# Inverses of an RWKV scan kept as packed 32-wide blocks, with the last level joining them to 64

## Chip, cores and metric

One NeuronCore of a Trainium2 chip runs the whole kernel as one launch. The metric is device time in microseconds.

## What is computed

The kernel runs a network of three blocks on 256 tokens of width 1024, in float32. The change lies in the second block's RWKV-7 mixer, with 16 heads of 64 features. What its scan must compute, cut to the core:

```python
def rwkv7_scan(r, decay, k, v, a, b):
    """State S[v_i, k_j]: S <- S diag(w) + (S a) b^T + v k^T ; y = S r."""
    def step(state, inp):
        r_t, w_t, k_t, v_t, a_t, b_t = inp
        sa = jnp.einsum('bhij,bhj->bhi', state, a_t)
        state = (state * w_t[:, :, None, :] + sa[..., None] * b_t[:, :, None, :]
                 + v_t[..., None] * k_t[:, :, None, :])
        y = jnp.einsum('bhij,bhj->bhi', state, r_t)
        return state, y
    _, y = lax.scan(step, s0, (r, decay, k, v, a, b))
```

The mixer calls it with `a = -kk` and `b = kk * a_rate`.

## The kernel before

The scan isn't stepped token by token. The 256 tokens are cut into four spans of 64. Within a span the rows `sa` depend on each other through a strictly triangular 64x64 matrix per head, and the kernel multiplies by the inverse of identity minus that matrix. There are 16 heads times 4 spans, so 64 such inverses. Two of them (two spans of one half of the tokens) lie above each other on the 128 partitions.

Inverses are made by doubling (`pe_double_a`, `pe_double_b`, L2254 to L2266; `dve_double_a`, `dve_double_b`, L2269 to L2280). The start is the inverse of the 2x2 blocks on the diagonal, `X`, and its transpose, `Y`. Level n joins blocks of size 2, 4, 8, 16 and 32 (`BLOCKS_64`) in three products: `between` is Lb by X, VectorE masks it into `T`; then `wider` is Y by T and is added to X, and `wider_turned` is T by Y and is added to Y. The last level makes only `wider_turned`, because the scan reads only `Y`. All products are 64x64 by 64x64, on full matrices that are zero outside their blocks.

The heads go in four groups of four, `pp` = 0 to 3. One call of `pe_blocks` (L2240) makes one product for one group: 16 calls of `mm`, over pair of heads q, token half b, head hd and span H, where H gives both the rows read and the partitions written. A float32 `mm` is two weight loads and two matmuls in the trace, so a call is 32 MATMUL and 32 LDWEIGHTS. The order is written by hand in `DOUBLING` (L2284): first product of group pp, then second and third of group pp-1, and so on, with four `bonus` products of another sum (L2295) put in between. All engines follow the same list, or their own share of it, in program order.

Ahead of it stand the pair products: `dve_front` (L2139) scales the operands, `pe_pairs` (L2159) makes Lb and Lk (64x128 each) and the 64x64 product for X, `dve_pairs` (L2198) masks them, GpSimd adds the unit diagonals (`pool_scan`, L2462), `pe_by_token` (L2224) transposes. Behind it `pe_span` (L2361) goes through the four spans one after the other and reads Y. TensorE, ScalarE and VectorE meet at the end of the scan (`all_drained`).

The trace names tiles by buffer: `rwkv_e_cum` holds X, `rwkv_e_neg_cum` holds Y, `rwkv_log_decay` holds T, `rwkv_pairs_b` is Lb. `L105` is the helper of all matmuls.

In block 3 another mixer has products of narrow tiles, that read 64 partitions, write 32 and have 32 columns (`pe_level`): 32 calls of `mm` for one level, so 64 MATMUL, with a wait only ahead of a level. `pe_mixers` has four such levels in a row (`LOW[0:4]`), and later two more.

## Time and profile before

| what | value |
|---|---|
| median of 3 runs | 3142.64 us (3137.49 to 3145.12) |
| the profiled execution | 3145.6 us, span 3143.8 us |
| TensorE | 2974.6 us busy (95%), 23720 MATMUL |
| weight loads | 2762.0 us busy, 23720 LDWEIGHTS |
| VectorE | 1718.4 us busy (55%) |
| ScalarE | 1435.3 us busy (46%) |
| GpSimd | 160.9 us busy (5%) |
| mean granted TensorE clock | 0.968 of full |

The RWKV scan takes the time from about 2338 us to 2464 us of the span: the pair products to 2369.9 us, the doubling to 2426.2 us, the spans to 2464.4 us. The rest of the kernel is large matrix products, which aren't touched.
### The profile page before, as it was taken

How to read it: one execution, taken by the hardware profiler on the slowest of the kernel's cores; microseconds unless marked ns; L12 is line 12 of the kernel's file. 1: busy time of each engine (PE TensorE's matmuls, PEld its weight loads, DVE VectorE, ACT ScalarE, POOL GpSimd, SP SyncE). 2: the span in 40 equal slices, each digit the busy share in tenths (PEclk: the TensorE clock that was granted, in tenths of full speed). 3: DMA queues.
4: the chain of work that ended last, by engine and by line, in shares of the span. 5: the costliest groups of instructions: out<-in, count | busy, mean ns of one | idle time of the engine just before them, and what ended most of it. 6: DMA issues, size and time to landing. Idle time of an engine off the chain costs nothing.

```text
span 3143.8 us, 53947 instructions
## 1 busy us (share of the span) xinstructions
PE 2974.6 (95%) x23720; PEld 2762.0 (88%) x23720; DVE 1718.4 (55%) x2029; ACT 1435.3 (46%) x1831; POOL 160.9 (5%) x197
## 2 busy tenths in 40 slices
PE   8998898999998898999999999999889999999998
PEld 8988898999988898998989899898879899886887
DVE  5464555545554555545555645545676454464555
ACT  4455655445455655444445444444451344344444
POOL 1000100000000100001000000000011000044000
PEclk9999999999999999999999999999889999898999
DMA  6553334554553334555554445454320155440453
GB/s 244 188 181 120 122 137 159 188 188 174 188 185 123 122 136 154 187 188 210 186 201 163 157 179 188 177 186 172 134 81 4 70 187 186 145 162 22 158 183 134
DMA packets 69395, 492.89 MB, mean 157 GB/s; under 512 B 7854, under 2 KB 9422, under 8 KB 10535
## 3 DMA queue, kind: packets, MB, share of 16 engines
q1 hardware_dynamic: 64224, 465.53, 41.2%
q10 hardware_dynamic: 4938, 23.92, 2.0%
q8 instruction: 188, 3.08, 0.4%
q14 instruction: 45, 0.36, 0.0%
HBM read 488.32 MB, written 1.06 MB: 156 GB/s over the span
## 4 chain that ended last, share of the span: by engine, by line
PE 80%; DVE 8%; ACT 6%; POOL 2%; issue 2%; PEld 1%; DMA 0%; PEldq 0%; ACTq 0%; DVEq 0%; POOLq 0%; SPq 0%
PE bank L105 52%; PE acc L105 28%; DVE weights_lo L313 2%; ACT weights_hi L118 2%; POOL conv_gate L3073 1%; POOL conv_out L3076 1%; DVE tmp L671 1%; DVE h L664 1%; DVE h L679 1%; PEld acc L105 0%; DVE b_x_lo L503 0%; PE acc L999 0%; DVE b_x_lo L731 0%; ACT L1067 0%; ACT L1133 0%
## 5 line engine op out<-in xcount | busy, mean ns | idle before, releaser
L313 DVE TENSOR_TENSOR weights_lo<-weight_ring,weights_hi 128x2048 fp32r<-128x2048 f32 x440 | 1009.6, 2295 | 944.8 <-ACT weights_hi L118 944.4
L105 PE MATMUL bank<-b_x_hi,weights_hi 128*128 128x256 f32 x3576 | 1015.8, 284 | 21.7 <-DVE b_x_lo L731 16.9
L105 PE MATMUL bank<-b_x_hi,weights_lo 128*128 128x256 f32 x3576 | 1011.1, 283 | 0.0
L118 ACT ACTIVATE weights_hi<-weight_ring 128x2048 fp32r<-128x2048 f32 x440 | 839.5, 1908 | 375.6 <-PE acc L105 364.7
L105 PE MATMUL bank<-b_x_lo,weights_hi 128*128 128x256 f32 x3576 | 1010.6, 283 | 0.0
L105 PEld LDWEIGHTS bank<-b_x_hi,weights_hi 128*128 128x128 f32 x3576 | 679.7, 190 | 34.3 <-issue 18.9
L105 PEld LDWEIGHTS bank<-b_x_lo,weights_hi 128*128 128x128 f32 x3576 | 680.0, 190 | 3.3
L105 PEld LDWEIGHTS bank<-b_x_hi,weights_lo 128*128 128x128 f32 x3576 | 679.1, 190 | 0.0
L105 PE MATMUL acc<-weights_hi,b_hidden_hi 128*128 128x512 f32 x832 | 329.5, 396 | 0.0
L105 PE MATMUL acc<-weights_hi,b_hidden_lo 128*128 128x512 f32 x832 | 328.2, 394 | 0.0
L105 PE MATMUL acc<-weights_lo,b_hidden_hi 128*128 128x512 f32 x832 | 327.5, 394 | 0.0
L118 ACT ACTIVATE b_hidden_hi<-act_gate 128x256 fp32r<-128x256 f32 x208 | 86.9, 418 | 340.0 <-DVE act_gate L888 312.4
L864 ACT ACTIVATE act_gate<-bank 128x256 f32<-128x256 f32 x176 | 67.6, 386 | 281.1 <-PE bank L105 280.9
L105 PEld LDWEIGHTS acc<-weights_hi,b_hidden_lo 128*128 128x128 f32 x832 | 156.5, 188 | 37.7
L105 PEld LDWEIGHTS acc<-weights_lo,b_hidden_hi 128*128 128x128 f32 x832 | 156.7, 188 | 32.8
L105 PEld LDWEIGHTS acc<-weights_hi,b_hidden_hi 128*128 128x128 f32 x832 | 156.5, 188 | 32.7 <-DVE weights_lo L313 0.4
L105 PE MATMUL bank<-weights_hi,b_x_hi 128*128 128x256 f32 (+2 forms) x528 | 152.8, 289 | 9.2 <-DVE weights_lo L313 7.6
L105 PE MATMUL bank<-weights_lo,b_x_hi 128*128 128x256 f32 (+2 forms) x528 | 152.4, 289 | 0.0
L105 PE MATMUL bank<-weights_hi,b_x_lo 128*128 128x256 f32 (+2 forms) x528 | 152.2, 288 | 0.0
L105 PE MATMUL acc<-b_x_hi,weights_hi 128*128 128x256 f32 x416 | 123.8, 298 | 16.5 <-ACT tmp L1067 11.3
L891 DVE TENSOR_TENSOR b_hidden_lo<-act_gate,b_hidden_hi 128x256 fp32r<-128x256 f32 x176 | 75.3, 428 | 85.2 <-ACT b_hidden_hi L118 85.2
L105 PE MATMUL acc<-b_x_lo,weights_hi 128*128 128x256 f32 x416 | 120.0, 289 | 0.0
(487 smaller groups left out, 4029.7 us busy)
## 6 DMA issues: line engine op xcount, KB each, us to landing
weight_ring<-in_weights SPq DMA_DIRECT2D x440, 1024.0 KB, 4.8
xn<-in_norm_rows ACTq DMA_DIRECT2D x14, 1024.0 KB, 4.8
sgu_bias_row<-in_sgu_rows ACTq DMA_DIRECT2D x1, 2048.0 KB, 10.8
sgu_norm_rows<-in_sgu_rows ACTq DMA_DIRECT2D x1, 2048.0 KB, 9.7
bias_hankel<-bias_scratch ACTq DMA_DIRECT2D x1, 1536.0 KB, 7.0
h<-in_x SPq DMA_DIRECT2D x2, 512.0 KB, 6.6
mem_norm<-in_memory SPq DMA_DIRECT2D x1, 1024.0 KB, 13.8
sgu_w_spatial<-in_sgu_w_spatial ACTq DMA_DIRECT2D x1, 1024.0 KB, 4.8
```

Source lines behind the costliest of these rows:

```text
L105: return pe.matmul(out, a, b, start=start, stop=stop, skip_group_check=True)
L118: return act.activation(out, in_, ACT.Copy, scale=scale)
L313: dve.tensor_tensor(k.w.lo[:, n % 2, :], k.ring[:, n % RING, :], k.w.hi[:, n % 2, :], ALU.subtract) \
L664: dve.scalar_tensor_tensor(out=h, in0=h, scalar=alpha / scale, in1=acc_of(k, b), op0=ALU.mult, op1=ALU.add, accum_out=stat(k, 0, b)).then_ ...
L671: dve.scalar_tensor_tensor(out=k.t[:, b], in0=k.h[:, b, :], scalar=stat(k, 1, b), in1=k.rows[:, 0], op0=ALU.add, op1=ALU.mult).then_inc(*k ...
L679: dve.scalar_tensor_tensor(out=half(k.h[:, b], i), in0=half(k.t[:, b], i), scalar=stat(k, 6, b), in1=half(k.rows[:, 1], i), op0=ALU.mult, ...
L864: act.activation(k.act_gate[:, c, :], k.bank[c][:, 0:S], ACT.Silu).then_inc(*k.s.up("silu", f, j, c))
L891: dve.tensor_tensor(k.hid.lo[:, j % 2, c, :], k.act_gate[:, c, :], k.hid.hi[:, j % 2, c, :], ALU.subtract) \
L3073: pool.tensor_scalar(k.conv_sg[:, 1, :], k.conv_in[:, 1, j:j + S], k.col(("conv_dw_w_3", (0, j)), 1), None, ALU.mult).then_inc(*k.s.up("po ...
L3076: pool.tensor_tensor(k.conv[:, 1, :], k.conv[:, 1, :], k.conv_sg[:, 1, :], ALU.add) \
```

## The change

`X`, `Y` and `T` are kept as packed 32x32 blocks: four blocks above each other on the partitions (`R4`), so X and Y together fill one buffer (`XY`, where X alone was), and T half of its old one. `pe_pairs` makes both start products as 32x32 tiles over 64 features (`pairs_32`, 64 calls of `mm` per group where `pairs_turned` had 16), VectorE masks them in one operation per head, and Y no longer comes from Lb. Levels n = 0 to 3 run all three products on 32x32 blocks, four `mm` per (q, b, hd) where there were two; VectorE's operations have 256 columns instead of 512. A last level (`last_a`, `last_b`) takes the quarter of Lb below the diagonal, multiplies it on both sides (two `mm` per (q, b, hd)), and the result is copied with the diagonal blocks into a full 64x64 transposed inverse `Y_64`, which lies in Y's old buffer and is zeroed by GpSimd before. ScalarE, VectorE and GpSimd share these copies. `pe_span` reads `Y_64`, and waits for the last of the copies just before the first use.

The diff, with unchanged lines left out:

```diff
+    "scalar_last": ("diagonal_act", "below_act", "right_act"),
+    "vector_last": ("below_dve", "right_dve", "mask_pairs"),
+    "gpsimd_last": ("unit_diagonal", "no_left", "diagonal_pool"),
...
-    mats["identity_64"] = i == j
...
-    mats["pairs_down"] = (i // 2 == j // 2) & (i > j)
-    mats["pairs_up"] = (i // 2 == j // 2) & (i < j)
-    for n in BLOCKS_64:
+    i, j = row % 32, np.arange(32)[None, :]
+    mats["identities_32"] = np.concatenate([i == j, i == j], axis=1)
+    mats["pairs_32"] = np.concatenate([(i // 2 == j // 2) & (i > j), (i // 2 == j // 2) & (i < j)], axis=1)
+    for n in BLOCKS_32:
...
-BLOCKS_64 = (2, 4, 8, 16, 32)
+BLOCKS_32 = (2, 4, 8, 16)
...
-    k.X, k.Y = by_head(k.eL[:, :, :]), by_head(k.emL[:, :, :])
+    k.XY = by_head(k.eL[:, :, :])
+    k.X, k.Y = k.XY[:, :, :, :, 0:32], k.XY[:, :, :, :, 32:64]
+    k.Y_64 = by_head(k.emL[:, :, :])
...
-    k.T = by_head(ld.rearrange("p (q t) -> p q t", q=KT))
+    k.T = ld[:, 1024:].rearrange("p (q b h t) -> p q b h t", q=KT, b=NB, h=2)
...
-        outs = [empty(k, pe, bank + hd, ("mask_up" if of == "b" else "mask_k", pp, hd))
+        outs = [empty(k, pe, bank + hd, ("mask_" + of, pp, hd))
...
-    outs = [empty(k, pe, hd, ("mask_down", pp, hd))[:, 0:S].rearrange("p (q b t) -> p q b t", q=2, b=NB)
+    outs = [empty(k, pe, hd, ("mask_pairs", pp, hd))[:, 0:S].rearrange("p (q b i t) -> p q b i t", q=2, b=NB, i=2)
...
-    for q in range(2):
-        for c in range(4):
-            b, H, T = span(c)
-            for hd in range(2):
-                a = mm(pe, outs[hd][H, q, b, :], k.rw["kk"][F2[hd], 2 * pp + q, T], k.rw["b"][F2[hd], 2 * pp + q, T],
-                       q + b == 0, True)
-    a.then_inc(*k.s.up("pairs_turned", pp))
-def identities(k, n):
-    return k.con("identity_64").unsqueeze(1).to_broadcast([P, n, 64])
+    kk, bb = k.rw["kk"], k.rw["b"]
+    for i, (x, y) in enumerate(((kk, bb), (bb, kk))):
+        for q in range(2):
+            for b in range(NB):
+                for R, T in tiles_32(b):
+                    for hd in range(2):
+                        a = mm(pe, outs[hd][R, q, b, i, :], x[F2[hd], 2 * pp + q, T], y[F2[hd], 2 * pp + q, T],
+                               i + q + b == 0, True)
+    a.then_inc(*k.s.up("pairs_32", pp))
+R4 = [slice(32 * r, 32 * r + 32) for r in range(4)]
+def tiles_32(b):
+    return [(R4[r], slice(b * P + 32 * r, b * P + 32 * r + 32)) for r in range(4)]
...
 def mask_64(k, name, n):
...
-        dve.tensor_tensor(one_half(k.Y, pp, hd), lb[:, :, 0:64], mask_64(k, "pairs_up", 4), ALU.mult) \
-            .then_inc(*k.s.up("mask_up", pp, hd))
...
-    dve.wait_ge(*k.s.at("pairs_turned", pp))
+    dve.wait_ge(*k.s.at("pairs_32", pp))
...
-        dve.tensor_tensor(one_half(k.X, pp, hd), k.bank[hd][:, 0:S].rearrange("p (n t) -> p n t", n=4),
-                          mask_64(k, "pairs_down", 4), ALU.mult).then_inc(*k.s.up("mask_down", pp, hd))
+        dve.tensor_tensor(one_half(k.XY, pp, hd), k.bank[hd][:, 0:S].rearrange("p (n i) -> p n i", n=4),
+                          mask_64(k, "pairs_32", 4), ALU.mult).then_inc(*k.s.up("mask_pairs", pp, hd))
...
 def of_two(x, pp):
...
-def pe_blocks(k, pe, bank, pp, mark, taken, lhs, rhs, *ready):
-    out = empty(k, pe, bank, taken).rearrange("p (q b h t) -> p q b h t", q=2, b=NB, h=2)
+def pe_blocks(k, pe, bank, pp, mark, taken, lhs, rhs, *ready, rows=R4, to=R4):
+    out = empty(k, pe, bank, *taken)[:, 0:S].rearrange("p (q b h t) -> p q b h t", q=2, b=NB, h=2)
...
-                for H in F2:
-                    a = mm(pe, out[H, q, b, hd, :], lhs(2 * pp + q)[H, b, hd, :], rhs(2 * pp + q)[H, b, hd, :],
+                for n, (R, O) in enumerate(zip(rows, to)):
+                    a = mm(pe, out[O, q, b, hd, :], lhs(2 * pp + q, n)[R, b, hd, :], rhs[R, 2 * pp + q, b, hd, :],
...
 def pe_double_a(k, pe, n, pp):
...
-    pe_blocks(k, pe, pp % 2, pp, ("between", n, pp), ("between_masked", n, pp), lambda px: k.Lb[:, px, :, :, 0:64],
-              lambda px: k.X[:, px], inverse(n, pp))
+    pe_blocks(k, pe, pp % 2, pp, ("between", n, pp), (("between_masked", n, pp),),
+              lambda px, r: k.Lb[:, px, :, :, 32 * (r % 2):32 * (r % 2) + 32], k.X, inverse(n, pp))
...
 def pe_double_b(k, pe, n, pp):
...
-    if n < len(BLOCKS_64) - 1:
-        pe_blocks(k, pe, 2 + pp % 2, pp, ("wider", n, pp), ("inverse", n + 1, pp), lambda px: k.Y[:, px],
-                  lambda px: k.T[:, px], ("between_masked", n, pp))
-    pe_blocks(k, pe, 4 + pp % 2, pp, ("wider_turned", n, pp), ("inverse_turned", n + 1, pp), lambda px: k.T[:, px],
-              lambda px: k.Y[:, px], ("between_masked", n, pp), *((("inverse_turned", n, pp),) if n else ()))
+    pe_blocks(k, pe, 2 + pp % 2, pp, ("wider", n, pp), (("inverse", n + 1, pp),), lambda px, r: k.Y[:, px], k.T,
+              ("between_masked", n, pp))
+    pe_blocks(k, pe, 4 + pp % 2, pp, ("wider_turned", n, pp), (("inverse_turned", n + 1, pp),),
+              lambda px, r: k.T[:, px], k.Y, ("between_masked", n, pp), *((("inverse_turned", n, pp),) if n else ()))
+def pe_last_a(k, pe, n, pp):
+    pe_blocks(k, pe, pp % 2, pp, ("below", pp), (("below_act", pp), ("below_dve", pp)),
+              lambda px, r: k.Lb[:, px, :, :, 32:64], k.X, inverse(N_DOUBLE, pp), rows=R4[0::2], to=R4[1::2])
+def pe_last_b(k, pe, n, pp):
+    pe_blocks(k, pe, 4 + pp % 2, pp, ("right", pp), (("right_act", pp), ("right_dve", pp)), lambda px, r: k.T[:, px],
+              k.Y, ("below_act", pp), ("below_dve", pp), ("inverse_turned", N_DOUBLE, pp), rows=R4[1::2], to=R4[0::2])
+def in_half_bank(bank):
+    return bank[:, 0:S].rearrange("p (n t) -> p n t", n=8)
...
 def dve_double_a(k, dve, n, pp):
...
-    dve.tensor_tensor(of_two(k.T, pp), k.bank[pp % 2].rearrange("p (n t) -> p n t", n=8),
-                      mask_64(k, f"down_{BLOCKS_64[n]}", 8), ALU.mult).then_inc(*k.s.up("between_masked", n, pp))
+    dve.tensor_tensor(of_two(k.T, pp), in_half_bank(k.bank[pp % 2]), mask_64(k, f"down_{BLOCKS_32[n]}", 8), ALU.mult) \
+        .then_inc(*k.s.up("between_masked", n, pp))
...
 def dve_double_b(k, dve, n, pp):
...
-        if come == "wider_turned" or n < len(BLOCKS_64) - 1:
-            dve.wait_ge(*k.s.at(come, n, pp))
-            dve.tensor_tensor(of_two(x, pp), of_two(x, pp), k.bank[bank + pp % 2].rearrange("p (n t) -> p n t", n=8),
-                              ALU.add).then_inc(*k.s.up(mark, n + 1, pp))
+        dve.wait_ge(*k.s.at(come, n, pp))
+        dve.tensor_tensor(of_two(x, pp), of_two(x, pp), in_half_bank(k.bank[bank + pp % 2]), ALU.add) \
+            .then_inc(*k.s.up(mark, n + 1, pp))
+def act_last_a(k, act, pp):
+    act.wait_ge(*k.s.at("inverse_turned", N_DOUBLE, pp))
+    for r in range(2):
+        copy_act(act, of_two(k.Y_64[:, :, :, :, 32 * r:32 * r + 32], pp)[R4[r]], of_two(k.Y, pp)[R4[r]]) \
+            .then_inc(*k.s.up("diagonal_act", pp, r))
+    act.wait_ge(*k.s.at("below", pp))
+    copy_act(act, of_two(k.T, pp)[R4[1]], in_half_bank(k.bank[pp % 2])[R4[1]]).then_inc(*k.s.up("below_act", pp))
+def act_last_b(k, act, pp):
+    act.wait_ge(*k.s.at("right", pp))
+    copy_act(act, of_two(k.Y_64[:, :, :, :, 32:64], pp)[R4[0]], in_half_bank(k.bank[4 + pp % 2])[R4[0]]) \
+        .then_inc(*k.s.up("right_act", pp))
+def act_last(k, act):
+    act.wait_ge(*k.s.at("no_left"))
+    for pp in range(4):
+        act_last_a(k, act, pp)
+        if pp:
+            act_last_b(k, act, pp - 1)
+    act_last_b(k, act, 3)
+def dve_last_a(k, dve, n, pp):
+    dve.wait_ge(*k.s.at("below", pp))
+    dve.tensor_copy(of_two(k.T, pp)[R4[3]], in_half_bank(k.bank[pp % 2])[R4[3]]).then_inc(*k.s.up("below_dve", pp))
+def dve_last_b(k, dve, n, pp):
+    if not pp:
+        dve.wait_ge(*k.s.at("no_left"))
+    dve.wait_ge(*k.s.at("right", pp))
+    dve.tensor_copy(of_two(k.Y_64[:, :, :, :, 32:64], pp)[R4[2]], in_half_bank(k.bank[4 + pp % 2])[R4[2]]) \
+        .then_inc(*k.s.up("right_dve", pp))
+def pool_diagonals(k, pool):
+    pool.wait_ge(*k.s.at("bonus_gated", 3))
+    for pp in range(4):
+        pool.wait_ge(*k.s.at("inverse_turned", N_DOUBLE, pp))
+        for r in range(2):
+            pool.tensor_copy(of_two(k.Y_64[:, :, :, :, 32 * r:32 * r + 32], pp)[R4[2 + r]],
+                             of_two(k.Y, pp)[R4[2 + r]]).then_inc(*k.s.up("diagonal_pool", pp, r))
+            pool.wait_ge(*k.s.at("diagonal_pool", pp, r))
+N_DOUBLE = len(BLOCKS_32)
...
-for _n in range(len(BLOCKS_64)):
+for _n in range(N_DOUBLE + 1):
...
-        DOUBLING.append(("a", _n, _pp))
+        DOUBLING.append(("a" if _n < N_DOUBLE else "last_a", _n, _pp))
...
-            DOUBLING.append(("b", _n - (_pp == 0), (_pp - 1) % 4))
-DOUBLING.append(("b", len(BLOCKS_64) - 1, 3))
+            _m = _n - (_pp == 0)
+            DOUBLING.append(("b" if _m < N_DOUBLE else "last_b", _m, (_pp - 1) % 4))
+DOUBLING.append(("last_b", N_DOUBLE, 3))
...
 def pe_span(k, pe, c):
...
+    if not c:
+        for m in (("right_act", 3), ("right_dve", 3), ("diagonal_pool", 3, 1)):
+            pe.wait_ge(*k.s.at(*m))
...
-            a = mm(pe, cols64(out, px)[H], k.Y[H, px, b, i, :], cols64(k.R[i], px)[H], px == 0, True)
+            a = mm(pe, cols64(out, px)[H], k.Y_64[H, px, b, i, :], cols64(k.R[i], px)[H], px == 0, True)
...
-        {"a": pe_double_a, "b": pe_double_b, "bonus": pe_bonus}[half](k, pe, n, pp)
+        {"a": pe_double_a, "b": pe_double_b, "last_a": pe_last_a, "last_b": pe_last_b, "bonus": pe_bonus}[half](k, pe, n, pp)
...
-    pe.wait_ge(*k.s.at("inverse_turned", len(BLOCKS_64), 3))
...
+    act_last(k, act)
...
-        {"a": dve_double_a, "b": dve_double_b, "bonus": dve_bonus}[half](k, dve, n, pp)
+        {"a": dve_double_a, "b": dve_double_b, "last_a": dve_last_a, "last_b": dve_last_b, "bonus": dve_bonus}[half](k, dve, n, pp)
...
 def inverse(n, pp):
-    return ("inverse", n, pp) if n else ("unit_diagonal", pp, "X")
+    return ("inverse", n, pp) if n else ("unit_diagonal", pp)
...
 def pool_scan(k, pool):
...
-        for x, name, come in ((k.Y, "Y", "mask_up"), (k.X, "X", "mask_down")):
-            pool.wait_ge(*k.s.at(come, pp, 1))
-            pool.tensor_tensor(of_two(x, pp), of_two(x, pp), identities(k, 8), ALU.add) \
-                .then_inc(*k.s.up("unit_diagonal", pp, name))
+        pool.wait_ge(*k.s.at("mask_pairs", pp, 1))
+        pool.tensor_tensor(of_two(k.XY, pp), of_two(k.XY, pp), mask_64(k, "identities_32", 8), ALU.add) \
+            .then_inc(*k.s.up("unit_diagonal", pp))
+    pool.memset(k.emL[:, :, :], 0.0).then_inc(*k.s.up("no_left"))
...
+    pool_diagonals(k, pool)
...
```

## Rows read from the trace of the kernel before

**Rows 1.** Busy time, granted clock and DMA by stage.

```profile
core 0: us, PE busy (x) PEld busy (x) DVE busy (x) ACT busy (x) POOL busy (x), PEclk, DMA share, GB/s
...
2340.00:2369.80 29.80, 21.66 (x432) 19.33 (x432) 25.55 (x54) 6.16 (x12) 11.23 (x8) 0.79 0.07 28
2369.80:2426.20 56.40, 56.40 (x1777) 54.45 (x1776) 39.98 (x58) 4.72 (x10) 5.10 (x4) 1.00 0.02 4
2426.20:2464.40 38.20, 36.45 (x937) 35.78 (x933) 10.36 (x16) 7.13 (x12) 0.00 (x0) 1.00 0.01 3
```

**Rows 2.** The chain that ended last: start us, us, what.

```profile
2358.02 0.60 DVE rwkv_pairs_b L2202
2358.62 0.33 DVE rwkv_e_neg_cum L2204
2358.95 0.60 DVE rwkv_pairs_b L2202
2359.55 0.34 DVE rwkv_e_neg_cum L2204
2359.89 0.14 issue
2360.03 3.69 PE acc L105 x64
2363.72 0.85 PE bank L105 x32
...
2369.95 3.11 PE bank L105 x96
2373.07 0.93 PE acc L105 x32
2374.00 1.87 PE bank L105 x64
...
2379.60 0.93 PE bank L105 x32
2380.53 1.06 PE acc L105 x4
...
2459.82 1.87 PE bank L105 x32
```

**Rows 3.** Groups by form in the doubling: busy us, mean ns, idle before.

```profile
L105 PE MATMUL bank<-rwkv_e_cum,rwkv_pairs_b 64*64 64x64 f32 x640 | 22.0, 218 | 0.0
...
L2271 DVE TENSOR_TENSOR rwkv_log_decay<-bank,cons 128x512 f32<-128x512 f32 x20 | 13.8, 692 | 9.8 <-PE bank L105 9.8
L2279 DVE TENSOR_TENSOR rwkv_e_neg_cum<-rwkv_e_neg_cum,acc 128x512 f32<-128x512 f32 x20 | 13.8, 689 | 5.0 <-PE acc L105 5.0
...
L2321 POOL TENSOR_TENSOR tmp<-tmp,rwkv_gate 128x512 f32<-128x512 f32 x4 | 5.1, 1274 | 32.7 <-ACT tmp L2313 32.7
```

**Rows 4.** Groups of VectorE by form in the pair products.

```profile
L2202 DVE TENSOR_TENSOR rwkv_pairs_b<-acc,cons 128x512 f32<-128x512 f32 x8 | 5.4, 679 | 0.3 <-PE acc L105 0.3
...
L2204 DVE TENSOR_TENSOR rwkv_e_neg_cum<-acc,cons 128x256 f32<-128x256 f32 x8 | 3.3, 410 | 0.0
L2212 DVE TENSOR_TENSOR rwkv_e_cum<-bank,cons 128x256 f32<-128x256 f32 x8 | 3.0, 409 | 0.0
```

**Rows 5.** Timeline of TensorE in block 3: start us, us, what.

```profile
2889.65 0.76 PE L105 MATMUL bank<-hgrn_q,hgrn_k 64*32 64x32 f32 x64
2890.26 1.69 PE L105 MATMUL bank<-xn 64*32 64x32 f32 x164
2893.96 0.34 PE L105 MATMUL bank<-xn 64*32 64x32 f32 x28 [2.01 <-issue]
2894.30 0.61 PE L105 MATMUL acc<-cmp_w_by_key,cmp_v 15*64 15x256 f32 x2
...
2901.65 0.81 PE L105 MATMUL bank<-xn 64*32 64x32 f32 x64 [0.36 <-issue]
2902.32 0.75 PE L105 MATMUL bank<-tmp 64*32 64x32 f32 x64
2903.03 0.39 PE L105 MATMUL acc<-tmp 64*64 64x64 f32 x6
```

**Rows 6.** What TensorE waited for there.

```profile
PE bank L105 <- issue: 2.0, 1, 2.0
```

**Rows 7.** DMA of that stretch in 40 slices of 0.2 us.

```profile
GB/s 0 0 0 0 0 0 0 0 0 0 82 0 0 0 0 0 0 0 0 0 0 0 0 0 0 0 0 0 0 0 82 0 0 0 0 0 0 0 0 0
DMA packets 2, 0.03 MB, mean 4 GB/s; under 512 B 0, under 2 KB 0, under 8 KB 0
...
q8 instruction: 2, 0.03, 1.9%
```

**Rows 8.** Busy time and granted clock around it.

```profile
2889.60:2892.00 2.40, 2.35 (x230) 2.19 (x229) 2.07 (x6) 2.22 (x3) 0.17 (x1) 1.00 0.03 7
2892.00:2893.96 1.96, 0.00 (x0) 0.00 (x0) 0.88 (x3) 1.93 (x3) 0.00 (x0) 1.00 0.00 0
2893.96:2896.00 2.04, 2.04 (x34) 1.06 (x33) 0.00 (x0) 2.02 (x3) 0.00 (x0) 0.77 0.04 8
2896.00:2900.00 4.00, 4.00 (x13) 2.31 (x12) 0.00 (x0) 0.00 (x1) 0.00 (x0) 0.50 0.00 0
```

**Rows 9.** The two packets of it, in windows of 0.2 us.

```profile
2891.20:2891.40 0.20, 0.20 (x39) 0.20 (x30) 0.20 (x2) 0.20 (x1) 0.00 (x0) 1.00 0.35 82
...
2895.20:2895.40 0.20, 0.20 (x2) 0.19 (x1) 0.00 (x0) 0.20 (x1) 0.00 (x0) 0.50 0.43 82
```

**Rows 10.** DMA queues in the doubling.

```profile
q8 instruction: 14, 0.23, 1.6%
```

**Rows 11.** DMA in 40 slices of 0.25 us, 2371 to 2381.

```profile
GB/s 0 0 0 0 0 0 0 66 0 0 0 0 0 0 0 0 0 0 0 0 0 66 0 33 0 0 0 0 0 0 0 0 0 0 0 0 66 0 0 0
...
q8 instruction: 3, 0.05, 1.9%
```

**Rows 12.** DMA in 40 slices of 0.5 us, 2404 to 2424.

```profile
GB/s 0 0 0 33 0 0 0 0 0 0 33 0 0 0 0 0 0 0 33 0 0 0 0 0 0 33 0 0 0 0 0 0 0 33 0 0 0 0 0 0
DMA packets 5, 0.08 MB, mean 4 GB/s; under 512 B 0, under 2 KB 0, under 8 KB 0
```

**Rows 13.** The page, its queue of instructions.

```profile
q8 instruction: 188, 3.08, 0.4%
```

## The prediction

> **What bounds the kernel now.** I read the page first: TensorE is busy for 95% of the span, so a change in the scan is worth what it does to TensorE's path. Then the busy time by stage: in the doubling (2369.8 to 2426.2 us) TensorE is busy for all 56.40 us at the full clock, VectorE for 39.98 us; in the pair products ahead of it TensorE for 21.66 of 29.80 us and VectorE for 25.55 us [rows 1]. The chain of waits agrees: in the doubling it lies on TensorE alone, 32 matmuls every 0.93 us, and at the end of the pair products on VectorE up to 2359.89 us [rows 2]. VectorE's operations of 692 and 689 ns wait for TensorE each time (9.8 and 5.0 us of idle time in groups of 20) [rows 3]. So the doubling is TensorE's, and its unit is the call: 32 MATMUL in 0.93 us, or 29.2 ns for one. That is the array's pace: a row of 32 matmuls of the same form on one tile (H fixed, both operands there) took 1.87 us, 58.4 ns for one [rows 2], and in the doubling two tiles run side by side.
>
> **What the change asks of TensorE.** Counts, from the code. Before, 56 calls (20 + 16 + 20) of 64 instructions (32 MATMUL and as many weight loads) are 3584, and the four bonus products add 32, so 3616. After: levels 0 to 3 are 4 x 4 x 3 = 48 calls of 32 `mm`, each four instructions: 6144. The last level is 8 calls of 16 `mm`: 512. With the bonus 6688. So the arithmetic falls and the instructions grow by 85%. The start products grow by 48 `mm` in each group, 192 instructions.
>
> *Array time.* The trace has no 32x32 tile. The nearest rows are the narrow products of block 3, with tiles of 64x32 and 32 columns: 64 of them start in 0.61 us (2889.65 to 2890.26), and 164 take 1.69 us less the tail of the last one, about 1.5 us [rows 5]. That is 9.2 to 9.5 ns for one, so a call of 64 would take about 0.60 us instead of 0.93. Four tiles of 32x32 instead of eight of 64x32 might be slower; if only two ran side by side, 14.6 ns for one (half of 29.2) would give 0.93 us again.
>
> *Instruction supply.* The same burst shows what I take for the real bound. Four levels of 64 matmuls stand in a row there, with a semaphore only ahead of each. The timeline has 64 + 164 = 228 of them, then 2.01 us with nothing, then the other 28 [rows 5]. The gap lies 36 matmuls into the fourth level, where the code waits for nothing, and the waits view puts it down to issue [rows 6]; the clock was at full speed when it began [rows 8]. 228 matmuls with their weight loads are 456 instructions. The page has 188 packets of the instruction queue q8 with 3.08 MB, so 16 KB for one [rows 13], and 47,440 matmuls and weight loads on TensorE are 252 for one packet; in the doubling it is (1777 + 1776) / 14 = 254 [rows 1, 10]. So a packet is a block of about 256 instructions of TensorE. In the stretch with the burst there are two packets, at 2891.2 and 2895.2 us [rows 7], each of which took 1.1 to 1.4 us (0.35 and 0.43 of 16 queues for 0.2 us) [rows 9]. My reading: TensorE holds the rest of one block and the next one, a further block is asked for when a block is entered, and it can be used one turnaround later. 456 is the rest of a block, 200, and a whole one. The second block was entered at about 2890.3 us (200 instructions into the burst at 4.7 ns, less what the queue runs ahead), and work went on at 2893.96 us: 3.7 us. In bounds: the two packets of the starved stretch are 4.0 us apart (3.8 to 4.2, slices of 0.2) [rows 7], and in today's doubling, which has no gap, they come 3.5 and 3.75 us apart (slices of 0.25) [rows 11] and on average 3.75 us (30 slices of 0.5 us for four steps) [rows 12]. So the turnaround is between 3.6 and 3.9 us; I take 3.75, near the gapless ones, as 3.7 comes out of the burst too. Today a block of 256 takes the array 128 x 29.2 ns = 3.74 us, just what the supply gives. After the change the array wants it in 128 x 9.4 ns = 1.2 us, and the supply decides.
>
> The Trainium skill ("Runtime: NRT & Kernel Launch", "Instruction fetch mechanics") says that instructions come in 16 KiB blocks of 256, fetched while the current block runs, with only two lines held, and that the fetch is therefore hidden. The block size agrees with the 16 KB of the rows; "hidden" does not agree with the 2.01 us gap. By that sentence the change would be the gain of the first rival.
>
> **The sum**, against the profiled execution of 3145.6 us (span 3143.8), which lies 3 us above the median of 3142.64:
> 1. Doubling. 6688 / 254 = 26.3 blocks. Up to the first boundary about 0.5 us, then 25 turnarounds of 3.75 = 93.75 us, then the rest of the last block at the array's pace, 1.0 us: 95.2 us, for 56.4 now: +38.8. With 3.6 it is 91.5 (+35.1), with 3.9 it is 99.0 (+42.6). The bonus products, 1.06 us each today [rows 2], disappear under it.
> 2. Pair products. VectorE loses the two masks of Y from Lb, 0.33 us each on the chain [rows 2], in each group; the mask of X and Y together has the same 128x256 as that of X alone (409 ns) [rows 4]. TensorE starts the last group when VectorE's masks of the third are done (2359.89): six masks less ahead of it, -2.0. Its start products are 128 narrow matmuls for 32 wide ones of 0.85 us [rows 2]: at 9.4 ns 1.2 us, at twice that, since the clock there is low, 2.4 us; I take +0.5 in all. The 256 instructions more than fit into the time of those groups. Together -1.5, between -2.0 and 0.
> 3. The clock. TensorE would work some 1.2 of each 3.75 us. After the 2 us gap of block 3 the granted clock was 0.77 and then 0.50, the lower level [rows 8]. Inside the doubling that costs nothing (even at 19 ns a block takes 2.4 us). But the spans would begin at the lower level: the first product of 1.87 us [rows 2] and what follows would take twice as long for a few us. +2, between 0 and +3.
> 4. VectorE's operations halve to some 410 ns [rows 4], hidden already. The last level's copies: ScalarE four and VectorE two small ones a group, at most 0.69 us each by the wider rows [rows 3]; a group of the last level has 128 instructions, 1.9 us of supply. GpSimd's eight copies: a 128x512 operation takes it 1.27 us [rows 3], so two copies are 2.6 us at most, and behind the last inverse six calls of 64 instructions (5.6 us) still come before the scan's first product, 1.87 us, and its outputs. Nil; if that cover were gone, up to +2. GpSimd's zeroing of `Y_64` comes before the bonus sums, 50 us early. Nil.
>
> +38.8 - 1.5 + 2 = **+39.3**: 3184.9 us for such an execution, 3182 us against the median.
>
> **Rivals.**
> - *Faster: the supply is no bound* (the gap had another reason, or more blocks are held when the stream is even). Then levels 0 to 3 take 48 x 0.60 = 28.8 us, the last level 8 x 0.47 = 3.7 (32 matmuls at 14.6 ns), the bonus 4.8: 37.3 for 56.4, -19.1, and -1.5: 3142.6 - 20.6 = 3122 us. It decides from a turnaround under 1.2 us. For it: today's doubling shows no gap at all. Against: the gap within a level, and a packet itself takes 1.1 us. Chance 0.13.
> - *A floor for each matmul*, whatever its width. At today's 29.2 ns a call of 64 takes 1.87 us: 48 x 1.87 + 8 x 0.93 + 4.8 = 102 us, +45.6, with -1.5 3187 us. Against it the 9.4 ns of block 3 [rows 5]. Chance 0.06. The Trainium skill ("TensorE: Matmul & The Clock Gate", "Back-to-back issue gap") states a floor of about 25 ns from start to start up to 64 columns; the 9.4 ns don't agree with it, and by it the time of a block would be 3.2 us and still be hidden under the supply.
> - *A deeper store or quicker supply*: four more blocks held at the start, or 2.5 to 3 us for a block when nothing else moves. That takes 10 to 25 us off: 3157 to 3172 us. Chance 0.08.
> - *The change doesn't do what it says*: the 32x32 tiles can't run side by side, or the copies of three engines stall the last level. One tile at a time would be 29.2 ns again, so the time of the second rival or some us more. Chance 0.03.
> - The forecast: 0.70.
>
> **How the numbers follow.** Forecast 3182, its own range 3175 to 3190 from the turnarounds of 3.6 and 3.9 us and the clock. To hold 8 in 10 the range takes in the deeper store and the floor: 3158 to 3196. A measurement of this kernel tells 0.3% (9.4 us) from no change. Faster: the first rival, 0.13. Within 0.3%: 0.03 (a supply so much quicker that it just balances). Slower: 0.84.
>
> **What would show it.** In the doubling: q8 packets 3.6 to 3.9 us apart with some 26 of them; TensorE in bursts of about 128 matmuls in 1.2 us with gaps of about 2.5 us put down to issue, inside calls as well as between them; busy share near a third, a clock that falls to 0.50; VectorE idle for most of it. The whole stage would be 91 to 99 us long. In the pair products the third group's masks should end 2 us sooner. Wrong, if calls of 64 matmuls follow each other every 0.6 us without gaps; then the supply isn't what stopped block 3. Wrong in another way, if the matmuls stand evenly 29 ns apart.

## The result and the profile after

| | before | after |
|---|---|---|
| median | 3141.93 us (3133.12 to 3145.12, 6 runs) | 3209.03 us (3188.01 to 3214.17, 6 runs) |
| the profiled execution, its span | 3145.6 us, 3143.8 us | 3188.01 us, 3186.2 us |
| mean granted clock | 0.968 | 0.957 |

After by before is 1.021 [1.0191, 1.023]: slower by 67 us, above the upper end of the predicted range. On another chip the same pair gave 1.0193 [1.0159, 1.0227] (first experiment below). The page of after, its engines and its queue of instructions (15 packets more than in [rows 13]):

```profile
PE 2978.8 (93%) x25640; PEld 2765.7 (87%) x25640; DVE 1703.8 (53%) x2021; ACT 1439.8 (45%) x1847; POOL 159.6 (5%) x202
...
q8 instruction: 203, 3.33, 0.4%
```

1920 MATMUL more, and TensorE is busy for 4.2 us more only, so the lost time is idle time. The windows of after by stage, with the columns of [rows 1] (pair products, doubling, spans; then the stretch at the lower clock, and what follows it):

```profile
2332.20:2369.80 37.60, 26.09 (x816) 22.58 (x816) 25.54 (x53) 8.29 (x18) 7.16 (x5) 0.76 0.08 31
2369.80:2469.40 99.60, 58.37 (x3345) 51.76 (x3344) 26.01 (x59) 10.65 (x25) 8.24 (x12) 0.59 0.02 4
2469.40:2515.00 45.60, 44.58 (x900) 44.04 (x896) 9.38 (x14) 6.89 (x12) 0.00 (x0) 0.77 0.01 3
2432.00:2490.00 58.00, 40.83 (x1469) 39.53 (x1459) 12.67 (x28) 8.68 (x20) 3.16 (x8) 0.50 0.02 4
2490.00:2515.00 25.00, 23.98 (x618) 23.46 (x616) 6.20 (x9) 4.15 (x7) 0.00 (x0) 0.99 0.01 3
```

The doubling is busy for 58 of 99.6 us where it was busy for 56.40 of 56.40 [rows 1]. With the same boundaries in every trace (from the first scaled copy of VectorE; from the last transpose, the first doubling product; from the first span product; to the last), in us:

| stage | before | after | difference |
|---|---|---|---|
| ahead of the scan | 2337.9 | 2332.2 | -5.7 |
| pair products | 32.0 | 37.6 | +5.6 |
| doubling | 57.4 | 99.6 | +42.2 |
| spans | 36.2 | 45.5 | +9.3 |
| behind the scan | 680.3 | 671.2 | -9.1 |

The scan costs 57 us. The profiled execution was 42.4 us slower because the untouched parts were 14.8 us shorter in it. TensorE's timeline at the start of the doubling and, after the "...", one call further on at the full clock:

```profile
2369.83 1.35 PE L108 MATMUL bank<-rwkv_e_cum,rwkv_pairs_b 32*32 32x32 f32 x128
2371.20 0.71 PE L108 MATMUL bank<-rwkv_log_decay,rwkv_e_cum 32*32 32x32 f32 x60
2374.09 0.26 PE L108 MATMUL bank<-rwkv_log_decay,rwkv_e_cum 32*32 32x32 f32 x4 [2.17 <-issue]
2374.21 1.08 PE L108 MATMUL acc<-rwkv_e_cum,rwkv_log_decay 32*32 32x32 f32 x64
2375.05 1.04 PE L108 MATMUL bank<-rwkv_e_cum,rwkv_pairs_b 32*32 32x32 f32 x59
2377.51 0.32 PE L108 MATMUL bank<-rwkv_e_cum,rwkv_pairs_b 32*32 32x32 f32 x5 [1.42 <-issue]
...
2397.14 0.74 PE L108 MATMUL acc<-rwkv_e_cum,rwkv_log_decay 32*32 32x32 f32 x64
2397.73 0.70 PE L108 MATMUL bank<-rwkv_e_cum,rwkv_pairs_b 32*32 32x32 f32 x49
```

This is the gap of [rows 5], again and again and in the middle of calls. From 2374.09 to the gap there are 4 + 64 + 59 = 127 matmuls, so 254 instructions: one block. A call of 64 starts 0.60 us behind the one before at the full clock (9.3 ns for a matmul) and 0.84 us behind it at the lower one (13.1 ns). A block of 127 matmuls takes the array 1.2 us at the full clock and 1.7 us at the lower one, and the next block comes 3.83 us after the last (below): the array is two to three times as quick as its supply. What TensorE waited for in the doubling, with total, times and longest in us:

```profile
PE bank L108 <- issue: 31.8, 16, 2.6
PE acc L108 <- issue: 8.8, 5, 2.2
PE acc L108 <- DVE rwkv_e_neg_cum L2339: 0.5, 1, 0.5
```

40.6 us of gaps at issue, about all of the stage's idle time. The DMA of 2400 to 2420 us in slices of 0.5 us shows packets 4.0, 4.0, 4.5 and 3.0 us apart; all 26 of the stage come 3.83 us apart on average:

```profile
GB/s 0 0 0 33 0 0 0 0 0 0 0 33 0 0 0 0 0 0 0 33 0 0 0 0 0 0 0 0 33 0 0 0 0 0 33 0 0 0 0 0
DMA packets 5, 0.08 MB, mean 4 GB/s; under 512 B 0, under 2 KB 0, under 8 KB 0
```

### The profile page after: what moved, and what is told of

Same layout as the page of the kernel before. It is cut to its first block, busy times and chain, and to the rows that moved or that the text cites. A ratio compares the mean times of both kernels' runs of the same rounds, so it can differ in the third digit from the quotient of the medians.

```text
span 3186.2 us, 57813 instructions
## 1 busy us (share of the span) xinstructions
PE 2978.8 (93%) x25640; PEld 2765.7 (87%) x25640; DVE 1703.8 (53%) x2021; ACT 1439.8 (45%) x1847; POOL 159.6 (5%) x202
## 3 DMA queue, kind: packets, MB, share of 16 engines
HBM read 488.19 MB, written 1.06 MB: 154 GB/s over the span
## 4 chain that ended last, share of the span: by engine, by line
PE 81%; DVE 8%; ACT 6%; issue 3%; PEld 1%; DMA 0%; POOL 0%; PEldq 0%; ACTq 0%; DVEq 0%; SPq 0%; POOLq 0%
PE bank L108 52%; PE acc L108 28%; DVE weights_lo L316 3%; ACT weights_hi L121 2%; DVE tmp L674 1%; DVE h L667 1%; DVE h L682 1%; PEld acc L108 0%; DVE b_x_lo L734 0%; DVE b_x_lo L506 0%; ACT L1070 0%; PE acc L1002 0%; ACT L1136 0%; DMA weight_ring<-in_weights 0%; ACT tmp L1070 0%
```

## The experiments

**The change again.** After, unchanged, on another chip.

> The changed kernel once more, for a second trace. Stage lengths in the first trace of it: pair products 37.6 us (31.9 before), doubling to the first product of the spans 99.6 us (57.4 before), spans 45.8 us (36.4 before). Supply theory (a block of 256 instructions of TensorE every 3.8 us bounds the doubling): the doubling is 97 to 102 us again, with q8 packets 3.8 us apart on average, and the spans 8 to 11 us longer than before. What the total differs from 3188 us comes from outside the scan, mainly from how long the granted clock is low in block 3. Rival (the supply's turnaround itself varies from run to run): the doubling differs by over 5 us from 99.6 in the direction of the total.

Measured: 3197.02 us (3193.72 to 3214.09, 4 runs) beside 3140.11 (13 runs), 1.0193 [1.0159, 1.0227]. Its trace has 39.1 / 100.3 / 45.3 us for pair products, doubling and spans, and 26 packets 3.83 us apart. The medians differ by 56.9 us and the scans of the traces by 59.1: on this chip the scan is the whole slowdown. The 10 us more of the first chip come up again below.

**Each doubling product in two halves of 32 columns**, in the kernel before: as many instructions as after, the old tiles.

```diff
-                for H in F2:
-                    a = mm(pe, out[H, q, b, hd, :], lhs(2 * pp + q)[H, b, hd, :], rhs(2 * pp + q)[H, b, hd, :],
+                for C in (slice(0, 32), slice(32, 64)):
+                    for H in F2:
+                        a = mm(pe, out[H, q, b, hd, C], lhs(2 * pp + q)[H, b, hd, :], rhs(2 * pp + q)[H, b, hd, C],
```

> The kernel before, with each product of the doubling made as two of 32 columns each: same tiles (64x64), same columns in all, twice the instructions (7168 and 32 of the bonus for 3584 and 32). Result the same. Supply theory: 7200 / 254 = 28.3 blocks at 3.83 us = 107 us for the doubling instead of 57.4, +50 us, and the spans begin at the low clock, +9: +59 us in all. Array theory (only tiles and columns count): +0 to +2 us. A floor of 25 ns for each matmul: 128 x 25... a call of 64 matmuls takes 1.6 us, +37 us, without gaps.

Measured: 3193.03 us (3191.07 to 3196.8), 1.0164 [1.0146, 1.0181]. The doubling took 110.3 us, near what the supply would give, but the timeline says otherwise:

```profile
2371.28 2.03 PE L105 MATMUL bank<-rwkv_log_decay,rwkv_e_neg_cum 64*64 64x32 f32 x64
2373.14 2.03 PE L105 MATMUL acc<-rwkv_e_neg_cum,rwkv_log_decay 64*64 64x32 f32 x64
```

No gap, 64 matmuls every 1.86 us, 29.1 ns for one, as with 64 columns. The clock was full throughout, and the spans kept their 36.2 us. So half the columns save nothing here. What stayed is the weight load of 64 columns, and I take that for the pace; no run shows it by itself. Since 29.2 ns for a matmul is also the pace of the supply, this run does not separate the two. It was a badly chosen one.

**Only the first head of each pair**, in after: half of the doubling's products are left out, so half of the inverses are not made.

```diff
-            for hd in range(2):
+            for hd in range(1):
```

> The changed kernel, with the products of the doubling and of the last level made for one of two heads only (hd 0), so half of the inverses are not made; VectorE's, ScalarE's and GpSimd's work is unchanged. 3360 instructions of TensorE in the doubling for 6688. Supply theory: 13.2 blocks, 12 turnarounds of 3.83 us and 2 to 4 us more: 48 to 51 us for 99.6, so 48 to 52 us off the changed kernel, with gaps put down to issue still in it. Rival (the chain from TensorE to VectorE and back, or the copies of the last level, bound the stage): the chain has as many steps as before, so under 15 us off.

Measured: median 3156.87 us (10 runs: 3140.29 to 3164.47, and one of 3446.37 that the ratio leaves out), 1.0041 [1.0023, 1.0059]; doubling 52.4 us for the 48 to 51 expected. What TensorE waited for in it:

```profile
PE bank L108 <- issue: 11.2, 6, 2.3
PE acc L108 <- issue: 8.8, 4, 2.5
PE acc L108 <- ACT rwkv_log_decay L121: 1.0, 1, 1.0
PE acc L108 <- DVE rwkv_log_decay L2332: 0.7, 1, 0.7
```

The chain of dependent products is as long as in after and the stage is half as long, with 13 packets 3.88 us apart; 1.7 us of waits for the last level's copies now show. A chain through VectorE is out. The kernel as a whole is only some 40 us under the 3197 of after beside it, and the profiled executions differ by 29 us, though the doubling lost 48. The trace shows where a part of that went: the spans took 53.3 us for 45.3. The clock stayed at 0.50 for 38 us of gapless products:

```profile
2429.40:2468.00 38.60, 38.47 (x550) 38.04 (x546) 5.93 (x9) 4.53 (x8) 0.00 (x0) 0.50 0.01 2
```

**Warm products ahead of the spans**, in after: 32 MATMUL of 128x128, which add nothing to the result.

```diff
+    pe_warm(k, pe, 16, 3)
     pe_values_64(k, pe, 0)
```

> The changed kernel with 16 dense products of 128x128 by the identity (results unused) between the last level and the spans, to raise the clock. Theory: the spans were 9.4 us longer only because the granted clock was 0.50 up to 2490 us. The 16 products (64 instructions, 32 matmuls) cost 3.5 to 4 us at the low clock, the clock rises soon after, and the spans take 36.4 to 39 us instead of 45.8: 3 to 6 us off in all, the doubling unchanged. Rival (the low clock stays as long whatever stands there): 4 us more.

Measured: 3195.45 us (3194.52 to 3197.05), 1.017 [1.0154, 1.0187], 1.6 us under after beside it (3193.72 to 3214.09), which is within the spread of the runs, where 3 to 6 us were expected. The timeline, and two windows behind it:

```profile
2473.81 5.57 PE L108 MATMUL bank<-cons 128*128 128x128 f32 x32
2479.30 2.02 PE L108 MATMUL bank<-rwkv_v_by_token,rwkv_pairs_k 64*64 64x64 f32 x31
```

```profile
2475.00:2485.00 10.00, 10.00 (x158) 9.88 (x157) 1.37 (x2) 1.18 (x2) 0.00 (x0) 0.88 0.01 3
2485.00:2515.00 30.00, 28.98 (x755) 28.46 (x752) 7.59 (x11) 5.34 (x9) 0.00 (x0) 1.00 0.01 3
```

The spans take 36.6 us for 45.3: with the full clock they are within 0.4 us of before, so their loss is the clock. The products cost 5.5 us to win back 8.7 in the trace; that the kernel is faster for it isn't shown.

**The start product in four pieces of 16 columns**, in the kernel before: 384 MATMUL more in the pair products, as many as the change adds there.

```diff
+            for i in range(4):
+                C, TC = slice(16 * i, 16 * i + 16), slice(T.start + 16 * i, T.start + 16 * i + 16)
                 for hd in range(2):
-                    a = mm(pe, outs[hd][H, q, b, :], ... k.rw["b"][F2[hd], 2 * pp + q, T],
+                    a = mm(pe, outs[hd][H, q, b, C], ... k.rw["b"][F2[hd], 2 * pp + q, TC],
```

> The kernel before, with the start product of each group in the pair products made as four of 16 columns for one of 64: the same columns, 64 calls of mm a group for 16, as many instructions more as the change adds there (192 a group). Nothing else differs. Supply theory: gaps put down to issue appear in the pair products of groups 1 and 3 as in the changed kernel (6.0 us in four gaps there), the stage takes 35 to 39 us instead of 32.0, and the doubling stays at 57 to 58 us: 3 to 8 us more in all. Rival (the change's longer pair products come from the low clock and the form 64x32 of the tiles): 0 to 1.5 us more.

Measured: 3148.16 us (3146.4 to 3152.24), 1.0034 [1.0022, 1.0046]; pair products 37.2 us, +5.2. The waits show one gap only:

```profile
PE bank L105 <- issue: 0.9, 1, 0.9
```

The timeline of the third group at the full clock, and the start of the fourth:

```profile
2357.53 2.28 PE L105 MATMUL bank<-rwkv_b,rwkv_kk_r 64*64 64x16 f32 x122
2359.61 0.33 PE L105 MATMUL acc<-rwkv_kk_r,rwkv_b 64*64 64x128 f32 x2
```

122 pieces in 2.08 us are 17 ns for one, with four tiles at work where the doubling has two; the 32 whole products took some 0.6 us. So most of the cost is the array again, 1.6 us a group and more at the lower clock (TensorE was busy for 30.7 us of the stage, for 21.8 before), and it first ate the 4.7 us for which TensorE had waited for VectorE ahead of the last group. A piece of 16 columns needs more array time than a 64x32 tile (9.3 ns), so this run says little on the change's own pair products.

**Only `between` in halves**, in the kernel before, with the edit of the first split for that product alone.

```diff
+                for C in ((slice(0, 32), slice(32, 64)) if mark[0] == "between" else (slice(0, 64),)):
```

> The kernel before, with only the first product of each level (20 of 56 calls) made as two of 32 columns. 4864 instructions and 32 of the bonus. Supply theory: 4896 / 254 = 19.3 blocks at 3.83 us = 74 us for the doubling instead of 57.4, so +16 to +17 us. Rival (narrow products cost more each, by their number, without a common supply): e2 had 56 such calls for +53 us, so 20 of them +19 us; the two differ in where the gaps stand: supply, spread over all calls, also the unsplit ones; the rival, in the split calls alone.

Measured: 3156.15 us (3151.43 to 3160.55), 1.006 [1.0045, 1.0076]; doubling 75.8 us, +18.4 = 20 calls x 0.92 us. In the timeline an unsplit call takes its old 0.93 us (2366.86 to 2367.79):

```profile
2365.89 1.13 PE L105 MATMUL bank<-rwkv_log_decay,rwkv_e_neg_cum 64*64 64x64 f32 x32
2366.86 1.10 PE L105 MATMUL acc<-rwkv_e_neg_cum,rwkv_log_decay 64*64 64x64 f32 x32
2367.79 0.42 PE L105 MATMUL bank<-rwkv_e_cum,rwkv_pairs_b 64*64 64x32 f32 x9
```

The cost sits in the split calls alone, and no gap stands in an unsplit one, as the rival said. So I take the split kernels to be bound by the array, and the gaps that I expected of the supply didn't come. The proof is not strong: both kinds of call go at 29.1 ns for a matmul, and 74 us were expected of the supply for the 75.8 measured, so by the times alone this run separates the two no better than the first split.

**The levels of block 3 apart**, in the kernel before: the four levels of [rows 5] in two pairs with other products between them. The instructions stay the same.

```diff
-    for i, n in enumerate(LOW[0:4]):
+    for i, n in enumerate(LOW[0:2]):
...
+    for i, n in enumerate(LOW[2:4]):
+        pe_level(k, pe, n, (2, 3), 128 * (i + 2))
```

> The kernel before, its scan untouched; in block 3 two of the four narrow levels come after the first of the two value products that followed them, so that 256 instructions of narrow products stand in a row twice instead of 512 once. Same work, same result. Supply theory: the gap of 2.01 us at 2892 us goes or shrinks, as the next block comes while the wider products run, and the clock there may stay high: 2 to 5 us less, 3135 to 3138 for 3140. Rival (the gap is a wait for data of block 3 that the trace doesn't show): the gap stays somewhere in the levels, no change.

Measured: 3135.55 us (3130.04 to 3142.58, 11 runs) for 3138.4 (16 runs), 0.9991 [0.9982, 0.9999]. The timeline, and the window of the stretch (granted clock 1.00; it was 0.80 in the same window of before):

```profile
2893.29 0.76 PE L105 MATMUL bank<-hgrn_q,hgrn_k 64*32 64x32 f32 x64
2893.90 0.75 PE L105 MATMUL bank<-xn 64*32 64x32 f32 x64
...
2897.31 1.35 PE L105 MATMUL bank<-xn 64*32 64x32 f32 x128
2898.59 1.51 PE L105 MATMUL acc<-b_att_w_by_key,v_sel_win 128*64 128x256 f32 x8
```

```profile
2889.00:2906.00 17.00, 15.61 (x488) 11.42 (x487) 8.24 (x15) 12.27 (x23) 2.09 (x3) 1.00 0.09 18
```

The same narrow products, spread out, have no 2.01 us gap and lose no clock; what is left are gaps of 0.37 and 0.31 us further on, the first of which before has too [rows 5]. The gap of [rows 5] goes with how many narrow products come in a row. A wait for data isn't out by this run alone, since two of the levels now come later; the doubling, with a gap every 127 matmuls, is the better evidence. The kernel is the quickest of the study, by 2.9 us, which is less than the 0.3% that two kernels' medians tell apart in a few runs; its interval ends just short of 1. A gain is likely, not shown.

**The kernel before once more**, one run beside these.

> The kernel before once more, for a second trace. Pair products 32 us, doubling 57.4 us, spans 36.2 us again within 1 us; what the total differs from 3143.8 us of span comes from outside the scan.

Measured: 3141.68 us; 32.0 / 57.4 / 36.2 us and 677.2 behind the scan. The stages of before repeat to 0.1 us in the scan and to 3 us behind it.

**Each product of the doubling with 64 columns**, in after: the moving block is read twice over, so the array has twice the columns for the same instructions, and VectorE reads the first half.

```diff
-                    a = mm(pe, out[O, q, b, hd, :], lhs(2 * pp + q, n)[R, b, hd, :], rhs[R, 2 * pp + q, b, hd, :],
+                    a = mm(pe, out[O, q, b, hd, :, :], lhs(2 * pp + q, n)[R, b, hd, :],
+                           rhs[R, 2 * pp + q, b, hd, :].unsqueeze(1).to_broadcast([32, 2, 32]),
```

> The changed kernel, with each product of the doubling and of the last level run over its 32 columns twice (64 columns into the bank, VectorE reads the first 32): the same instructions and tiles, twice the columns of matmul. Result the same. Supply theory: the array's bursts get longer (128 matmuls in 1.9 us at the full clock, 3.4 us at the low one, both under 3.83), the gaps shorter, the doubling stays at 99 to 102 us; the clock may stay higher, and the spans then take 36 to 45 us: 0 to 10 us less than the changed kernel, in no case more than 2 us more. Rival (pace and gaps belong to the array or to its 32x32 tiles): 16 to 40 us more.

**Each product of the doubling in two of 16 columns**, in after: the same columns with twice the instructions.

```diff
+                    for C in (slice(0, 16), slice(16, 32)):
+                        a = mm(pe, out[O, q, b, hd, C], lhs(2 * pp + q, n)[R, b, hd, :], rhs[R, 2 * pp + q, b, hd, C],
```

> The changed kernel, with each product of the doubling and of the last level made as two of 16 columns: twice the instructions (13344 with the bonus), the same columns. Weight loads of 32 columns on four tiles, which e2 and e6 show to set the pace of split products, took no more than 13.4 ns each in the bursts of the changed kernel at the low clock. Supply theory: 13344 / 254 = 52.5 blocks, 51.5 turnarounds of 3.83 us and 4 us more: 201 us for the doubling, 100 us more than the changed kernel. Rival (weight loads or matmuls pace it): at most 48 x 128 x 13.4 ns + 8 x 64 x 26 ns + 8 = 104 us, 0 to 5 us more.

Measured: twice the columns 3190.53 us (3183.68 to 3215.28), 1.0179 [1.0124, 1.0234], doubling 97.9 us. Twice the instructions 3291.38 us (3281.97 to 3304.93), 1.0491 [1.0454, 1.0528], doubling 186.6 us with 52 packets 3.59 us apart. The same 80 us (2372 to 2452; the doubling begins at 2373.4, 2373.7 and 2370.9 us) in the windows of after on the second chip, of twice the columns, and of twice the instructions:

```profile
2372.00:2452.00 80.00, 47.73 (x2703) 41.69 (x2705) 20.08 (x45) 5.54 (x12) 5.88 (x6) 0.61 0.02 4
```

```profile
2372.00:2452.00 80.00, 53.18 (x2747) 47.48 (x2749) 20.50 (x46) 5.73 (x13) 5.87 (x6) 0.93 0.02 5
```

```profile
2372.00:2452.00 80.00, 47.47 (x2852) 43.51 (x2844) 11.10 (x25) 1.89 (x5) 2.53 (x2) 0.52 0.02 5
```

Matmuls of 32, 64 and 16 columns, at clocks of 0.61, 0.93 and 0.52, come at 29.6, 29.1 and 28.1 ns for one: columns and clock move the pace by 5%, and twice the instructions take 1.9 times as long. It is not the array's pace. Within the bursts, at the full clock, calls of twice the columns and of twice the instructions go like this:

```profile
2405.11 1.10 PE L108 MATMUL bank<-rwkv_log_decay,rwkv_e_cum 32*32 32x64 f32 x64
2406.03 0.83 PE L108 MATMUL acc<-rwkv_e_cum,rwkv_log_decay 32*32 32x64 f32 x43
```

```profile
2370.88 1.99 PE L108 MATMUL bank<-rwkv_e_cum,rwkv_pairs_b 32*32 32x16 f32 x189
2374.86 0.85 PE L108 MATMUL bank<-rwkv_e_cum,rwkv_pairs_b 32*32 32x16 f32 x64 [1.99 <-issue]
```

64 columns take 14.4 ns for a matmul and 16 columns 9.5, for the 9.3 of 32 columns. So with twice the columns the array works longer on a block, and what that takes comes out of the gaps (31.7 us in the doubling, for 41.0 of after on the second chip). All three stop for issue after a first run of 188 or 189 matmuls and then after every 127 or 128, or twice that. This pair decides for the supply. The spans behind twice the columns took 45.3 us, the upper end of what was expected. Twice the instructions took 186.6 us for 201, as a block came every 3.59 us and not every 3.83. That the weight load sets the pace of split products, as that expectation has it of the two split runs, they don't show; that 16 columns take as long as 32 here fits it.

**Without Y's start product**, in after: the second half of the new pair products is left out, so Y starts from stale values.

```diff
-    for i, (x, y) in enumerate(((kk, bb), (bb, kk))):
+    for i, (x, y) in enumerate(((kk, bb),)):
```

> The changed kernel, with the start product for Y left out in the pair products (the one for X stays; Y starts from what lies in the bank, so the inverses are not right): 32 calls of mm a group for 64, 128 instructions less in each of four groups. Supply theory: the four gaps of 6.0 us in all in the pair products shrink to 0 to 2 us, the stage takes 32 to 35 us for 37.6, the doubling stays at 99 to 102 us. Rival (the stage is longer by the low clock alone): 1 to 1.5 us less, gaps as before.

Measured: 3189.63 us (3181.18 to 3206.94), 1.0171 [1.0135, 1.0206]; pair products 28.8 us for the 32 to 35 expected, 3.2 us less than before the change; doubling 96.5 us for 99 to 102. Its waits at issue in that stage:

```profile
PE bank L108 <- issue: 0.4, 1, 0.4
```

With 256 narrow MATMUL the pair products gain 3.2 us, with 512 they lose 5.6. It is not the gaps alone that went: TensorE was busy for 20.2 us of the stage, for 26.1 in after, and waited 2.7 us for VectorE again. Beside it, what TensorE waited for in the pair products of after:

```profile
PE bank L108 <- issue: 3.5, 2, 2.1
PE acc L108 <- issue: 2.5, 2, 1.4
```

**Four more traces of after**, for the difference between its runs.

> The changed kernel as it is, for its trace. Its times go from 3188 to 3214 us, and both traces so far are of times near the lower end (3188 and 3194 us), where stages are: pair products 37.6 and 39.1, doubling 99.6 and 100.3, spans 45.5 and 45.3 us. Theory (clock): in the executions near 3210 us the doubling is the same within 2 us, and the granted clock stays low for longer behind it, so that the spans take 55 to 70 us. Rival 1 (supply): the turnaround is longer there, the doubling takes 110 us or more. Rival 2 (elsewhere): all three stages are as in the first traces and the 20 us lie outside the scan.

Measured, in us:

| run | time | pair products | doubling | spans | behind the scan | of it at the lower clock |
|---|---|---|---|---|---|---|
| after | 3188.01 | 37.6 | 99.6 | 45.5 | 671.2 | 61 |
| again | 3193.72 | 39.1 | 100.3 | 45.3 | 672.3 | 66 |
| third | 3191.97 | 38.4 | 97.1 | 45.5 | 674.5 | 68 |
| fourth | 3196.86 | 37.3 | 96.9 | 45.3 | 677.7 | 82 |
| fifth | 3203.08 | 38.4 | 98.6 | 44.8 | 682.2 | 87 |
| sixth | 3194.66 | 37.5 | 97.9 | 44.7 | 677.3 | 82 |

None of the four reached 3210 us. In the longest, 3203.08 us, the spans took 44.8 us where the clock theory wanted 55 to 70, and the doubling 98.6 where the rival of the supply wanted 110 or more, so the third reading is the one that fits.

The scan takes 179.5 to 184.7 us in all six, 54 to 59 us more than the 125.6 of before. The spread between runs lies behind the scan, in code that was not touched, and goes with the time at the lower clock there. The unprofiled runs say the same by their span and mean clock: 3186.2 us at 0.957, 3196.0 at 0.952, 3212.3 at 0.948. Twice the missing share of the clock is the time at the lower level: 274, 307 and 334 us. So 60 us more of it go with 26 us more of time, 0.43 us for one. The median run of the result (3207 us at about 0.9495) had some 324 us; before has 195 (3140.1 us at 0.969). The scan accounts for 107 of these 129 us (18 + 82 + 21 for 14). The other 22 us at 0.43 are 10 us, and 57 + 10 = 67. That is an estimate: no run of 3207 us or more has a trace, and why the untouched parts lose more clock in some runs, and in most of the first chip's, stays open.

## Why the prediction was right or wrong

*What bounds it.* Right. The gaps are at issue and inside calls, the packets 3.7 to 3.9 us apart on average and 26 in number, VectorE is idle for most of the stage, and twice the columns with the same instructions cost nothing. The rival with no supply bound (3122 us) is out by the gaps, the floor for each matmul by 9.3 ns in the bursts, the quicker supply by the packets. (In the sums of the first two rivals the four bonus products are 4.2 us at 1.06 each, not 4.8.) The Trainium skill ("Runtime: NRT & Kernel Launch", "Instruction fetch mechanics") has the fetch hidden; 40.6 us of gaps in one stage say that it is hidden only while a block's work takes longer than its turnaround.

*Step 1, doubling.* +38.8 predicted, +42.2 in the profiled execution, +39.5 to +42.9 over the six. The term that was too small is the turnaround: 3.83 us for 3.75, which is 2.0 of the 3.4 us in 25 blocks. The last block ran at 13.1 ns for a matmul instead of 9.4 (0.5 us), and the wait for a copy of the last level is 0.5 us. The 56.4 us of [rows 1] end 1.1 us ahead of the first product of the spans, so against the whole stage the 95.2 us of the sum are 4.4 short; the remaining 1.4 us stay open. The four later traces, with 3.72 to 3.78 us, took 96.9 to 98.6 us. That 3.75 came so near is partly luck: the distances that it was taken from are those of a doubling without gaps, where blocks can come no faster than the array works them off (128 x 29.2 ns = 3.74 us), and they say no more than that the supply keeps up with that. What measured the supply was the burst of block 3, with 3.7 us, and its two packets, 4.0 us apart.

*Step 2, pair products.* -1.5 predicted, +5.6 measured, and this step failed. "The 256 instructions more than fit into the time of those groups" looked at the stage's mean and not at its bursts: 128 narrow MATMUL of one group are a whole block that the array works off in 1.2 to 1.7 us. Four gaps of 1.1 to 2.1 us, 6.0 us in all, follow. They stand where before had 4.7 us of waiting for VectorE ahead of the last group, so TensorE's idle time grew by 1.3 us only. The other 4.3 us are busy time, 26.1 us for 21.8, where the step had "+0.5 in all": the start products took 1.2 to 1.5 us a group for 0.6 to 1.1 (2.2 us more in all), and 18 us of the stage are at the lower clock for 14. Without half of the narrow start products the stage is 8.8 us shorter: 5.6 us of gaps and 5.9 us of busy time less, and 2.7 us of waiting for VectorE back. There the saving of masks shows as the step had it: the last group starts 20.2 us into the stage for 22.2, 2.0 us sooner. The prediction's own theory, applied to this stage as it was to the doubling, would have given the gaps.

*Step 3, the clock.* +2 predicted, +9.3 measured: right in kind, too small by the time the lower level lasts. The spans work without a gap from 2469.4 us, yet the clock stays at 0.50 up to about 2490. I had put "a few us". Nor is 20 us a constant: with one head it was 38 us. Two groups of the spans, before and then after (line, tiles, count; busy us, mean ns):

```profile
L105 PE MATMUL bank<-rwkv_v_by_token,rwkv_pairs_k 64*64 64x64 f32 x128 | 8.3, 219 | 0.0
```

```profile
L108 PE MATMUL bank<-rwkv_v_by_token,rwkv_pairs_k 64*64 64x64 f32 x128 | 11.5, 267 | 0.0
```

20.6 us at half speed lose 10.3, about what the stage lost, and the warm products give back 8.7 of it.

*Step 4, the copies and VectorE.* Right. VectorE's operations take 424 ns, and of the last level's 32 copies one is waited for, 0.5 us. Two groups of after in the doubling:

```profile
L2295 DVE TENSOR_TENSOR rwkv_log_decay<-bank,cons 128x256 f32<-128x256 f32 x16 | 6.8, 424 | 26.6 <-PE bank L108 26.4
...
L2339 DVE COPY rwkv_e_neg_cum<-acc 32x256 f32<-32x256 f32 x3 | 1.3, 422 | 2.0 <-PE acc L108 2.0
```

*The total.* The sum gave 3184.9 us for the profiled execution and it took 3188.01, but that agreement is partly luck: the scan was 57 us longer, not 39, and the untouched parts 14.8 us shorter. The six runs' median, where that luck is gone, is above the range. Two terms had too narrow bounds, the pair products (up to 0) and the clock (up to +3), and in both a starved supply has its part: by gaps in the pair products, beside the array's longer work there, and by the clock in the stage behind. The three steps together were 17.8 us short (57.1 for 39.3). The some 10 us from there to the median lie outside the scan, and why they do stays open.

## What to carry to other kernels

Count instructions in a row and not columns: in this kernel TensorE gets one block of 256 instructions (128 MATMUL with their weight loads) every 3.6 to 3.9 us on average, so a run of some 190 to 230 MATMUL that take less than 29 ns each ends in a stall, however little they compute. Test each stage for it by bursts, not by its mean; then add the stages behind, which start at the lower clock. Where small products can't be avoided, put large ones between them: the levels of block 3 lost their gap by it, and in the doubling of after TensorE ran 253 or 254 matmuls without a gap where a bonus product lay among them. Smaller tiles save arithmetic, but here they cost 85% more instructions in a stage that then waited for instructions.
